# Placing the expert slots of the prompt tile by VectorE's free time, and scaling the attention's exponentials on ScalarE

## What is computed

```python
h = rms_norm(x) * (1 + scale1) + shift1
gates, za, zb, zq, zkv, kpe = split(h @ w_in)
ya = chunk_gating_mlp(za)                 # A
yb = hyena_branch(zb)                     # B: short conv, then a long convolution by transforms
yc = latent_attention(zq, zkv, kpe, past) # C: 8 heads, softmax over 512 own (+ 128 past) keys
merged = sum over A, B, C of sigmoid(gate) * (y @ w_branch)
x = x + g1 * (merged @ w_out)
h2 = rms_norm(x) * (1 + scale2) + shift2
x = x + g2 * peer_ffn(h2)                 # 8 heads x top 16 of 128*128 single-neuron experts
```

## Time and profile before

| what | value |
|---|---|
| median of three runs | 4969.43 us |
| the profiled execution's own time | 4967.44 us |
| its span, first to last instruction | 4965.6 us |
| PE (TensorE matmul) busy | 3999.7 us, 81% |
| DVE (VectorE) busy | 3199.5 us, 64% |
| POOL (GpSimd) busy | 2531.8 us, 51% |
| ACT (ScalarE) busy | 623.6 us, 13% |
| mean granted TensorE clock | 0.914 of full |
| DMA | 1621.66 MB, mean 327 GB/s |

### The profile page before, as it was taken

One profiled execution on the slowest core, in us unless ns is written; L12 is line 12 of the kernel. 1 busy time (PEld: TensorE's weight loads), 2 busy tenths in 40 slices (PEclk: granted clock), 3 DMA queues, 4 the chain that ended last, 5 costly groups with the idle time before them and its releaser, 6 DMA issues.

```text
span 4965.6 us, 39614 instructions
## 1 busy us (share of the span) xinstructions
PE 3999.7 (81%) x12079; PEld 2067.3 (42%) x12079; DVE 3199.5 (64%) x7543; ACT 623.6 (13%) x1286; POOL 2531.8 (51%) x2570
## 2 busy tenths in 40 slices
PE   8877577959988989788879856797798898777777
PEld 4543234735554433344343422374455443322223
DVE  0257798386566765566655788855856678676763
ACT  1131032110001000101100302311100000100000
POOL 0004556136555655466555355541565666677774
PEclk9888678989999999899999967798899999999999
DMA  8547778669999999999999487784899999999997
GB/s 274 173 142 277 281 258 302 219 239 373 397 376 365 377 378 393 353 395 381 395 366 362 166 300 256 264 309 167 329 399 379 358 391 375 385 410 389 403 408 298
DMA packets 591362, 1621.66 MB, mean 327 GB/s; under 512 B 52064, under 2 KB 218544, under 8 KB 589874
## 3 DMA queue, kind: packets, MB, share of 16 engines
q0 software_dynamic: 368640, 1342.34, 71.2%
q1 hardware_dynamic: 221938, 276.62, 16.3%
q10 hardware_dynamic: 576, 0.16, 0.0%
HBM read 1616.16 MB, written 2.79 MB: 326 GB/s over the span
## 4 chain that ended last, share of the span: by engine, by line
PE 32%; DMA 29%; DVE 19%; POOL 9%; issue 5%; DVEq 2%; SPq 1%; ACT 1%; PEldq 0%; PEld 0%; ACTq 0%; POOLq 0%
DMA rows<-in_peer_u_dram,idx 21%; PE ps L1393 13%; PE ps L927 10%; POOL rows L2275 8%; DVE rows L2167 6%; DMA rows<-in_peer_v_dram,idx 3%; PE ps L934 3%; DVE work L2209 3%; PE ps L897 2%; DMA ring<-in_w_in_dram 2%; DMA work<-in_peer_v_dram,idx 1%; DMA ring<-in_w_ada_dram 1%; SPq L753 1%; POOL work L2275 1%; DVE work L1989 1%
## 5 line engine op out<-in xcount | busy, mean ns | idle before, releaser
L2275 POOL DMA_INDIRECT rows<-in_peer_u_dram,idx x1280 | 1250.2, 977 | 1407.2 <-DVE dots L2167 578.1
L2167 DVE CUSTOM_DVE_ANT_0 rows<-rows,ps 128x1024 f32<-128x1024 f32 x1024 | 1247.4, 1219 | 961.8 <-DMA rows<-in_peer_u_dram,idx 952.0
L1393 PE MATMUL ps<-rows,work 128*128 128x512 f32 x2736 | 1289.3, 608 | 224.6 <-DMA rows<-in_peer_v_dram,idx 198.4
L2275 POOL DMA_INDIRECT rows<-in_peer_v_dram,idx x940 | 960.3, 1022 | 775.1 <-DVE work L2209 341.9
L1393 PEld LDWEIGHTS ps<-rows,work 128*128 128x128 f32 x2736 | 503.6, 193 | 921.7 <-issue 769.3
L1393 PE MATMUL ps<-work 128*128 128x512 f32 x1360 | 653.6, 613 | 100.6 <-DMA work<-in_peer_v_dram,idx 79.1
L927 PE MATMUL ps<-h_s,ring 128*128 128x256 f32 (+1 forms) x1792 | 460.8, 416 | 29.6 <-DMA ring<-in_w_in_dram 17.0
L1393 PEld LDWEIGHTS ps<-work 128*128 128x128 f32 x1360 | 251.9, 194 | 444.7 <-issue 368.1
L2275 POOL DMA_INDIRECT work<-in_peer_v_dram,idx x340 | 320.5, 943 | 222.1 <-PE ps L1393 144.8
L927 PEld LDWEIGHTS ps<-h_s,ring 128*128 128x128 f32 x1792 | 343.7, 193 | 150.3 <-issue 91.2
L2167 DVE CUSTOM_DVE_ANT_0 rows<-rows,work 128x1024 f32<-128x1024 f32 x256 | 312.5, 1224 | 133.5 <-DMA rows<-in_peer_u_dram,idx 122.6
(11 more groups left out here) (292 smaller groups left out, 3374.9 us busy)
## 6 DMA issues: line engine op xcount, KB each, us to landing
ring<-in_w_in_dram SPq DMA_DIRECT2D x92, 1024.0 KB, 11.3
ring<-in_w_ada_dram SPq DMA_DIRECT2D x48, 1024.0 KB, 12.7
ring<-in_peer_wq_dram SPq DMA_DIRECT2D x48, 1024.0 KB, 11.6
ring<-in_w_out_dram SPq DMA_DIRECT2D x24, 1024.0 KB, 6.1
rows<-in_peer_u_dram,idx POOLq DMA_INDIRECT x1280, 7.7
rows<-in_peer_v_dram,idx POOLq DMA_INDIRECT x940, 7.5
ring<-in_tables_dram SPq DMA_DIRECT2D x10, 1024.0 KB, 8.4
ring<-in_w_branch_c_dram SPq DMA_DIRECT2D x16, 512.0 KB, 8.6
```

The source lines that it names most:

```text
L1393: mm = pe.matmul(y_acc[:, cols], diag[:, e % TOPK, :], v_row_of(t, e)[:, cols], start=e == 0, stop=e == EXPERTS - 1)
L2167: dve.tensor_tensor_reduce(rows[:, s, :], rows[:, s, :], tok, 1.0, 0.0, ALU.mult, ALU.add, dots[:, e:e + 1]).then_inc(rows_u_free, 1)
L2275: pool.indirect_dma_start(to, None, table, bass.IndirectOffsetOnAxis(ap=idx[:, t % 2, e:e + 1], axis=0)).then_inc(came, 16)
```

## The change

It does four things.

1. The prompt tile's slots are spread by new tables (`spare`, `slot_work`, `prompt_cuts`) in place of `mix_share` with S_SHARE. `spare` is, per place, a TensorE time less a VectorE time (at least a tenth of the TensorE time). `slot_work` is a VectorE time per slot: 2.3 us for a selection part, 1.35 for a dot product, 1.4 more where a row of `peer_v` is added. Slots go by the running sum of both.
2. In the sample's attention ScalarE multiplies the 640 exponentials of step m - 1, after the exponentials of step m. VectorE makes only the sum and the reciprocal, and releases a new semaphore `share_ready`.
3. ScalarE copies the prompt tile's tokens in slots 1 and 3 instead of 0 and 1.
4. Everything else, the number of slots among it, stays.

By these tables the places that move most are (slots that TensorE's order has ahead of the place, the same in both layers):

| place | before | after |
|---|---|---|
| filt2 | 4 | 1 |
| u, first | 25 | 22 |
| conv, first | 32 | 37 |
| mix, first | 56 | 50 |
| cos, first | 57 | 54 |
| rope | 79 | 67 |
| step 0 | 79 | 68 |
| step 16 | 105 | 83 |
| gate, first | 138 | 102 |
| gate, group 2 | 152 | 127 |
| out, first | 166 | 154 |
| out, third | 171 | 164 |
| out, fourth | 174 | 174 |

```diff
--- before.py
+++ after.py
@@ -363,9 +363,49 @@
 
 
 PROMPT_SLOTS = GROUPS * PARTS + EXPERTS + W_LAG + 8
+
+
+def spare(i, name):
+
+    kind = name if isinstance(name, str) else name[0]
+    width = i.W / SAMPLE
+    tensor = {"qk": 5.6, "v": 3.5, "u": 6.9, "conv": 6.9, "filt3": 0.9, "mix": 4.3, "cos": 3.4, "sin": 3.4, "idft": 6.9,
+              "step": 4.0, "gate": 6.9, "branch": 2.3, "out": 6.9, "norm1": 6.9, "norm2": 6.9 * width,
+              "q": 1.7, "Ka": 0.9, "rope": 0.9}.get(kind, 0.5)
+    vector = {"filt1": 5.0, "filt2": 5.0, "norm1": 9.0, "norm2": 9.0 * width, "conv": 2.8, "filt3": 1.8, "mix": 0.7,
+              "sin": 2.7, "at": 1.2, "idft": 2.0, "step": 2.2, "branch": 1.2, "out": 1.0}.get(kind, 0.0)
+    if name == ("v", i.NT - 1):
+        vector = 4.5
+    if name == ("hyt", 0):
+        vector = 2.5
+    return max(tensor - vector, 0.1 * tensor)
+
+
+def slot_work(n):
+
+    n -= GROUPS * PARTS
+    if n < 0:
+        return 2.3
+    return (1.35 if n < EXPERTS else 0.3) + (1.4 if W_LAG <= n < EXPERTS + W_LAG else 0)
+
+
+def prompt_cuts(l, instances):
+
+    names = [(i, name) for i in instances for name, _ in turn_order(i)
+             if not (i.kind == "S" and name[0] in ("Sa", "Sb", "Ta", "Tb", "V", "q", "Ka", "Kb", "Y"))]
+    total, work = sum(spare(*n) for n in names), sum(slot_work(n) for n in range(PROMPT_SLOTS))
+    o, room, done, slot = [], 0, 0, 0
+    for i, name in names:
+        while slot < PROMPT_SLOTS and done + slot_work(slot) <= room / total / SPREAD * work:
+            done += slot_work(slot)
+            slot += 1
+        o.append((slot_of(l, False, slot), PLACE[i, name]))
+        room += spare(i, name)
+    return o
+
+
 SAMPLE_SLOTS = STILES * EXPERTS + 40
 SPREAD = 0.97
-S_SHARE = 0.77
 FIRST_SLOT = -PARTS
 
 
@@ -387,10 +427,7 @@
     o = [(0, PLACE[SAMPLES[0], "begin"] - 1)] * 4
     for l in range(LAYERS):
         s, (g0, g1), (q0, q1) = SAMPLES[l], GATES_S[l], QUERIES_S[l]
-        for i, lo, hi in ((s, 0, S_SHARE), (g0, S_SHARE, 1)):
-            for place, share in mix_share(i):
-                share = (lo + share * (hi - lo)) / SPREAD
-                o.append((slot_of(l, False, min(PROMPT_SLOTS, int(share * PROMPT_SLOTS))), place))
+        o += prompt_cuts(l, (s, g0))
         done = slot_of(l, False, PROMPT_SLOTS)
         o += [(done, PLACE[q0, "begin"] - 1)] * 4
         o += [(done, PLACE[q0, ("key", 0, 0)])] * 2
@@ -698,6 +735,7 @@
         kpe_ready = signal("kpe_ready", P=1, S=1)
         max_ready = signal("max_ready", P=2, S=PAIRS)
         exp_ready = signal("exp_ready", P=2, S=PAIRS)
+        share_ready = signal("share_ready", S=PAIRS)
         prob_ready = signal("prob_ready", P=2, S=PAIRS)
         merged_ready = signal("merged_ready", P=1, G=1)
         fin_ready = signal("fin_ready", F=1)
@@ -1631,6 +1669,10 @@
                         if j == STILES - 1:
                             act.wait_ge(exp_ready.sem, exp_ready.after(i, m + 1))
                             act.sem_inc(bank_taken[TURN[i, ("Sb", h)][0]], 1)
+                    if 0 <= m - 1 < PAIRS:
+                        probs, col = v.prob[:, (m - 1) % 2, :], (m - 1) % 4
+                        act.wait_ge(share_ready.sem, share_ready.after(i, m))
+                        act.activation(probs, probs, ACT.Copy, scale=stat[:, 3, col:col + 1]).then_inc(prob_ready.sem, 1)
                     if h + 1 < HEADS and j == 2:
                         take_keys(h + 1, "Ka", 0, SAMPLE)
                     if h + 1 < HEADS and j == 3:
@@ -1718,7 +1760,7 @@
             def prompt_tile(l):
                 t = tile_of(l, False)
                 for half in range(2):
-                    yield slot_of(l, False, half)
+                    yield slot_of(l, False, 2 * half + 1)
                     act.wait_ge(swap_full, SWAP[t, f"tok{half}"] + 1)
                     act.copy(tok_p[:, half * 512:(half + 1) * 512], swap).then_inc(swap_taken, 1)
                 for group in range(GROUPS):
@@ -2027,10 +2069,7 @@
                         dve.wait_ge(exp_ready.sem, exp_ready.after(i, before + 1))
                         dve.tensor_tensor(share, total, stat[:, 2, col:col + 1], ALU.add)
                         dve.drain()
-                        dve.reciprocal(share, share)
-                        dve.drain()
-                        probs = v.prob[:, before % 2, :]
-                        dve.tensor_scalar(probs, probs, share, None, ALU.mult).then_inc(prob_ready.sem, 1)
+                        dve.reciprocal(share, share).then_inc(share_ready.sem, 1)
                     if m < PAIRS:
                         col = m % 4
                         a = full(i, ("Sa", m))
```

## The result

| | median us | runs |
|---|---|---|
| before, measured alongside | 4964.27 | 4958.91 to 4972.47 |
| after | 4940.41 | 4927.38 to 4944.15 |

By the medians the change makes the kernel 24 us faster, 0.48%. The ratio of the mean times is 0.9944, with an interval of 0.9927 to 0.9962, which is 0.56% or 28 us; either way it is faster by more than the runs scatter. The forecast was 4921 us, 48 us less than the median then known. The profiled execution took 4944.15 us with a span of 4942.3 us.

What follows compares the result with a forecast made beforehand. VectorE was taken to bound the attention, VectorE and gathers the transforms, TensorE most gates. Per layer 2 + 132 + 152 + 176 + 66 = 528 us against 550.9 and 553.4, giving 4921 us, range 4845 to 4995.

Steps and rivals of the forecast that it cites:

- start: Ahead of slot 38: selection parts and the first `conv` trade places; between -2 and +5 us, taken as +2.
- the loop: Addition frees a buffer, `peer_v` gather, `peer_u` gather behind it, dot product, addition: 10.4 us per three slots, 3.48 each.
- VectorE over 80% busy: Sign expected in the gates' profile: VectorE busy over 80%, with waits for `peer_u` rows.
- TensorE waiting for VectorE's evacuations: Sign expected in the gates: TensorE waits for banks that VectorE frees late, at a lower clock.
- rival A: More gain than forecast: gates at 3.5 us a slot, attention 140 us, 490 us a layer, 4845 us; chance 0.17.
- I take 132: Convolutions and transforms with 32 slots: 132 us instead of 180.6, between 120 and 148; gathers seldom bind.
- four buffers, 2.4 us a row: Tail: 18 additions behind slot 147 at 2.4 us make 43 us of its 66 us.
- 4.45 us a step, with 34 of them: Attention: engine chain and VectorE's 4.0 us step disturb each other, giving 152 us; high end 176 us.
- The round of 4.2 us: Attention step as a chain of scaling, transposes, their copies, exponentials and handovers: 4.2 us, scaling 0.75 of it.
- The low end of the attention, 137 us: Attention: 209.1 us less 72, for 20 slots (51 us) and the multiplications leaving VectorE.
- B, the gather stream fixes the time: Slot 38 to 147: all 110 slots keep their pace, 442 us; no gain, 4969 us; chance 0.18.
- C, the round: Attention: next scores join the engine chain, 5.6 us a step, 5002 us; slower from 5.2 on; chance 0.13.

Runs made afterwards that it cites:

- E4: The changed kernel with `V_LAG_P` 17 instead of 16, so a `peer_v` gather stands one place later in GpSimd's program; 4882.5 us, ratio 0.9834.
- E8: The changed kernel with ScalarE scaling only the first of the 640 columns, the rest left unscaled; 4909.62 us, ratio 0.9877.
- E1: The changed kernel with the new slot placement but VectorE scaling the exponentials as before; 4920.47 us, ratio 0.991.
- E3: The changed kernel with ScalarE's scaling of step m - 1 ahead of the exponentials of step m instead of behind them; 4902.86 us, ratio 0.987.
- E6: The changed kernel with ScalarE's scaling ahead of the exponentials and `V_LAG_P` 17 instead of 16; 4843.81 us, ratio 0.9745.
- E10: The changed kernel with ScalarE's scaling ahead of the exponentials and `V_LAG_P` 18 instead of 16; 4849.59 us, ratio 0.9756.

## Why the prediction was right or wrong

The sign was right, the time lay in the range (4845 to 4995 us), and the gain was half of the forecast.

| layer 0, us | forecast | measured |
|---|---|---|
| start | +2 | -1.5 |
| transforms | 132 | 137.5 |
| attention | 152 | 168.2 |
| gates, 45 slots | 176 (3.9 each) | 176.9 (3.93 each) |
| tail | 66 | 58.2 |
| sum | 528 | 539.3 |

The attention alone was missed by 16 us and the transforms by 5.5. The sum is only 11 us off because the start and the tail came out 11 us better than forecast, and that was luck.

**Gates: right in size, and the loop as its cause.** The slot at 3.9 us was taken between the loop's 3.48 (10.42 us over three slots are 3.47) and the measured 4.05, and E4 confirms that the loop paces it: one slot more of lookahead and the slot costs 3.53 us. Two signs that the forecast added were wrong. VectorE over 80% busy: it works 120.75 of 176.9 us, 68%, and that figure did not follow from the sum's own 3.9 us a slot, of which the two expert instructions are only 2.5. And TensorE waiting for VectorE's evacuations: the clock was lower, 0.84, but TensorE waited for the gate weights, 24.3 us. (The "15 slots" at 4.05 us that rival A is held against are the 13 of the earlier trace rows.)

**Transforms: 5.5 us too little.** "I take 132" lay between VectorE's work, 120, and that plus the old waits, 148. The waits for rows are 12.6 us; E4 takes 11.4 us off by lookahead. So here too the loop bound more than "seldom".

**Tail: 8 us better**, on the term "four buffers, 2.4 us a row". 58.2 us hold the rest of the additions, the last out and the norm.

**Attention: the step that failed.** The forecast put "4.45 us a step, with 34 of them". The 31 rounds from the first step's score matmul (570.1 us) to the last step's (719.2) took 149.1 us, 4.81 each, and what lies after them 19.1 us instead of three steps' 13.4. Against 34 x 4.45 = 151.3 us that is 31 x 0.36 = 11 us in the rounds and 6 in the end. The price of the scaling was estimated at 0.75 us and measured at 0.83; by E8, where 0.54 us of instruction were worth 0.5 us of step, those 0.08 us explain some 2 or 3 us. The larger part is the mean. The round of 4.2 us was built for an ordinary step, and ordinary steps are faster (3.9 us in the mean). The fourth step of each head, where TensorE makes values and queries first, was not worked out; it takes 5.5 to 9.1 us, 7.6 in the mean. Since the transposes wait for the last thing ScalarE does in a step, TensorE has no lead from the three short steps to spend there. That last sentence is read from the order of time; E1 and E3, which give TensorE the transposes' input sooner, agree with it by 10 and 21 us, but they shorten every kind of step.

**A sign taken wrong inside the sum.** The low end of the attention, 137 us, counts VectorE's multiplications as 21 us saved (18.3 busy, 2.8 ahead). Without that the forecast's own sum leaves 209.1 less 51, 158 us, and E1 measured 158.1. So its 152 expected 6 us from moving the scaling; where the change puts it, it costs 10 instead (168.2), and 20 us over the whole kernel. That difference of 16 us is the attention's miss. The change is two things of opposite sign: the slots bring 49 us (E1), as much as the forecast's whole gain, and the scaling gives back 20. Of the words of the Trainium skill that the prediction weighed (ScalarE: Activation LUTs, Rules for kernel authors: mul belongs on VectorE) the trace agrees for this placement. It doesn't for E3's, 17.6 us faster than VectorE's own scaling in E1.

**The rivals.** A (gates at 3.5 us, attention at 140) did not come, but E6 reaches its time, 4843.81 us against the 4845 worked out, with gates of 152 and an attention of 147. The loop's lookahead and the order on ScalarE are what lay between. B, the gather stream fixes the time: the tail shrank by 51 us, so the time was not fixed, but its mechanism, the gather stream, is what paces the gates. C, the round: its mechanism was there, transposes waiting for ScalarE's scaling (34.7 us), at 4.8 us a step and not 5.6, so below the 5.2 from which it decides. The first attention matmul came at 570.1 us (forecast 568), the last dot product at 912.4 (897, and not past 920), Q's at 973.4 (962).

**The bytes.** The prediction set the trace's 388 GB/s over 35 us against the 358 GB/s of the Trainium skill (DMA: Bandwidth & Descriptors, Where 436 GB/s comes from). E4, E6 and E10 hold 385 to 391 GB/s for about 150 us. Here the measurement decides: these gates are not held to 358 GB/s. Whether 390 is their bound stays open with E10.

**What stays open.** The share of the fourth step in the attention's 16 us was read from the order of time and not tried by itself. Nor was a fifth row buffer, which should do what the lag does and go past it, and which alone could show whether the gates of E6 are at the limit of the bytes.

## What to carry to other kernels

Moving an operation to an engine with time to spare makes a step longer if it becomes the last link before the next engine's work. Ask behind what it stands in that engine's order, and put it where the engine would wait anyway: here the same instruction cost 20 us at the end of ScalarE's step and was worth 18 us at its head. When two streams of gathers share one in-order queue, count how many uses ahead the second can be issued while the first waits for its buffer; one constant was worth 58 us, more than twice the change. And when a mean step time is built from a chain, build it for each kind of step, since the rare long one is hidden only by a lead that the chain must leave.

## What the runs showed of the hardware

ScalarE took 830 ns to scale 128x640 fp32 values in place (VectorE 571 ns) and 294 ns for a single column, so 0.84 ns a column and a fixed part of about 0.29 us. One core's DMA queues moved 385 to 391 GB/s for some 150 us (E4, E6, E10). ScalarE's load of a function table took 1.28 us, and the next activation started right behind it (648.93 to 650.22 us in the kernel after).

A gather's instruction on GpSimd takes 0.94 us as a rule, and up to 1.9 when it begins inside a dot product of VectorE. In the gates of the kernel after 28 gathers do, and 27 of them end 0.87 to 0.89 us after VectorE went on to its next instruction. The one at 781.73 ends at 783.37, VectorE went on at 782.48; the one at 529.01 in the earlier trace rows ends at 530.91, VectorE went on at 530.02. None of the 60 others takes over 1.0 us. It looks as if a gather that begins inside a dot product stands until that is over. This was read from the order of time, not tested by a run.
